# Moving the two split-weight buffers of a hybrid decoder layer by 80 bytes in SBUF

## The chip, the core and the metric

The kernel runs on one core of a Trainium2 chip. The metric is the device time of one launch in microseconds (us). Most runs of a kernel agree within 0.3%.

## What the reference computes

One inference step of a one-layer decoder, for 256 prompt tokens and 8 sample tokens (264 columns in all), in float32. The work is nearly all matrix products with weights that are read once:

```
x <- LN(a*x + 0.5*FFN1(x)); x <- LN(a*x + Mixer(x)); x <- LN(a*x + 0.5*FFN2(x))
swiglu(x) = (silu(x @ w_gate) * (x @ w_up)) @ w_down      # 2048 -> 5632 -> 2048
z = x @ w_in                                              # 2048 -> 10240: q,k,v | conv B,C,h | two gates
merged = sigmoid(g_attn) * (o @ w_attn_out) + sigmoid(g_conv) * (c_b*conv @ w_conv_out)
Mixer = merged @ w_o
```

Attention with two softmax maps per head, over the prompt and over a paged cache of 1024 positions for the 8 samples, lies between.

## The kernel before, in words

**Layout.** Features lie on the 128 partitions and the 264 tokens along each partition. An activation is a stack of tiles of 128 x 264 float32, 1056 bytes a partition each. Tile number kt is the kt-th block of 128 features.

**Split products.** Every float32 value is split into a high part of type float32r and a low remainder, and a product is made of three matmuls (`products`, lines 650 to 652): high weights by high activations (L650), high weights by low activations (L651), low weights by high activations (L652). The weight block, 128 x 128, is the stationary operand: its load is a record of its own (PEld), and the load for the next matmul runs beside the current matmul. The activation tile, 128 x 264, is the moving operand. So while one matmul streams its 264 columns out of one SBUF address, the load of the next reads 128 columns out of another.

**Weight pipeline.** Weights come in chunks of 256 rows x 512 columns (`KC` = 2 row blocks, `MC` = 4 column blocks), 512 KB each, by DMA from SyncE into the ring `w_raw` of 4 slots. ScalarE rounds a chunk into `w_hi` (L1004), VectorE subtracts and writes `w_lo` (L1382), TensorE runs 24 matmuls on it and then frees the slot (`w_used`). There are 752 chunks. A panel is a run of chunks that fills four PSUM banks: 8 chunks for products with x or m, 22 for the down projections (tiles `h_hi`, `h_lo`), 4 with `yc` or `o`. Within a chunk the order is row block, column block, the three products; in the last chunk of a panel column block comes first. The slot of a chunk is its running number modulo 4.

**Stages in order.** FFN1 gate and up: first the two panels side by side, chunk by chunk in turn (`side_by_side`, 16 chunks), then 20 panels one after another; down (4 panels with h); the query columns of `w_in` in two panels on activations not yet normalized (`first_panels`, tile `raw`, L764 to L766, 266 columns, 1064 bytes a tile); the rest of `w_in` with attention between; `w_conv_out` (tiles `yc`); `w_attn_out` (tiles `o`); `w_o` (tiles `m`); FFN2, which starts with two `raw` panels and then has 20 panels with x; down (4 panels with h). The two LayerNorm sums use small matmuls with the tile `ones`.

**Addresses.** A helper `at` places tensors one behind another at multiples of 32 bytes. The base that the allocator gives is byte 16,481 of the partition, so `x_hi` is at 16,512, `x_lo` at 33,408, `w_raw` at 50,304, `lam_in` at 66,688. Then `w_hi` is at 66,720 and `w_lo` at 83,360. A row of the split rings (one slot, one row block) is 512 columns and a gap of `W_GAP` = 8 columns that nobody uses, 2080 bytes. Later come small constants and LayerNorm tiles, and from `area`, rounded up to a multiple of `LINE` = 128 bytes, the large reused region: `h_hi` at 110,720, `h_lo` at 157,312, `m_hi` at 115,328, `o_hi` at 160,640, `raw` at 195,264, `yc_hi` at 202,752, `yc_lo` at 219,648. The matmuls read a weight block at

```
wh, wl = w_hi[:, s, k, m * P:(m + 1) * P], w_lo[:, s, k, m * P:(m + 1) * P]
```

that is at the ring's start + 2080 x (2s + k) + 512 m for slot s, row block k, column block m.

Of the kernel before, what the change touches and what calls it, by code (L numbers as in the profile page):

```python
# [20 lines left out]
F32R = mybir.dt.float32r  # L21
# [3 lines left out]
P = 128  # L25
# [5 lines left out]
HEADS, HD, VD = 8, 64, 128  # L31
# [3 lines left out]
KC, MC = 2, 4  # L35
RING = 4
LEAD = 3
WARM = 10
WC = MC * P
# [19 lines left out]
HEAD_STATS = 22  # L59
LATE = DT - MC  # L60
RAW = N + 2
LINE, W_GAP = 128, 8

class Count:
# [48 lines left out]
def program(nc, a, out):  # L114
    with ExitStack() as ctx:
# [4 lines left out]
        top = nc.sbuf_base  # L120
        end = nc.sbuf_usable_end

        def at(name, shape, dt=F32, offset=None):

            nonlocal top
            size = int(np.prod(shape[1:])) * 4
            if offset is None:
                top = -(-top // 32) * 32
                offset, top = top, top + size
            assert offset + size <= end, (name, offset, size, end)  # L130
            return nc.alloc_sbuf_tensor_at(name, shape, dt, offset=offset)
# [6 lines left out]
        y_norm = at("y_norm", [P, DT, N], F32, x_at + DT * TILE)  # L138
        w_raw = at("w_raw", [P, RING, KC, WC])
        lam_in = at("lam_in", [HD, 4])  # L140
        SPLIT_RING = RING * KC * (WC + W_GAP)
        w_at = -(-(top - 32) // LINE) * LINE + 32

        def spaced(flat):

            return flat[:].rearrange("p (s k n) -> p s k n", s=RING, k=KC)[:, :, :, 0:WC]

        w_hi = spaced(at("w_hi", [P, SPLIT_RING], F32R, w_at))
        w_lo = spaced(at("w_lo", [P, SPLIT_RING], F32R, w_at + SPLIT_RING * 4))
        top = w_at + (2 * SPLIT_RING - W_GAP) * 4  # L150
        lam_prod = at("lam_prod", [HD, 2])
        lam = at("lam", [P, 4])
        ident = at("ident", [P, P])
        ones = at("ones", [P, P])
        mask = at("mask", [P, 3, P])
# [53 lines left out]
        top = area  # L209
# [24 lines left out]
        top = max(top, zv_at + 6144 + (2 * PAD + SPLIT_COLS) * 4)  # L234
# [1820 lines left out]
```

## Time and profile before

| | |
|---|---|
| time, median of 3 runs | 2261.94 us (2261.67 to 2263.02) |
| the profiled execution: its own time | 2261.67 us |
| its span, first to last instruction | 2259.8 us |
| TensorE (PE) busy | 2243.9 us, 99% of the span |
| VectorE (DVE) / ScalarE (ACT) / GpSimd (POOL) busy | 1365.9 / 996.5 / 29.7 us |
| granted TensorE clock, mean | 0.998 of full |
| HBM read | 468 MB, 209 GB/s over the span |

Matmuls are pipelined: a matmul's record lasts some 280 ns, while the next one starts some 120 ns after it. What a matmul costs is the distance from start to start, which has to be read from start times; busy time does not show it.

### The profile page before, as it was taken

How to read it: one execution, taken by the hardware profiler on the slowest of the kernel's cores; microseconds unless marked ns; L12 is line 12 of the kernel's file. 1: busy time of each engine (PE TensorE's matmuls, PEld its weight loads, DVE VectorE, ACT ScalarE, POOL GpSimd, SP SyncE). 2: the span in 40 equal slices, each digit the busy share in tenths (PEclk: the TensorE clock that was granted, in tenths of full speed). 3: DMA queues.
4: the chain of work that ended last, by engine and by line, in shares of the span. 5: the costliest groups of instructions: out<-in, count | busy, mean ns of one | idle time of the engine just before them, and what ended most of it. 6: DMA issues, size and time to landing. Idle time of an engine off the chain costs nothing.

```text
span 2259.8 us, 45670 instructions
## 1 busy us (share of the span) xinstructions
PE 2243.9 (99%) x18574; PEld 2212.8 (98%) x18574; DVE 1365.9 (60%) x1523; ACT 996.5 (44%) x1236; POOL 29.7 (1%) x59
## 2 busy tenths in 40 slices
PE   9999999999999999999999999999999999999997
PEld 9999999999999999999998899999999999999997
DVE  5545454444655689999975447896444544445554
ACT  5444444433444454454543454554444434433333
POOL 1000000000000001000000000000000000000001
PEclk9999999999999999999999999999999999999999
DMA  7656666565555688989988855556656565655553
GB/s 246 195 177 186 179 183 183 176 188 181 182 180 182 189 283 291 318 290 323 331 310 312 296 182 189 185 175 189 181 176 189 174 191 176 186 185 180 179 185 114
DMA packets 233439, 475.47 MB, mean 210 GB/s; under 512 B 18448, under 2 KB 21888, under 8 KB 233312
## 3 DMA queue, kind: packets, MB, share of 16 engines
q1 hardware_dynamic: 225920, 465.22, 63.7%
q0 software_dynamic: 2320, 5.68, 0.8%
q10 hardware_dynamic: 5072, 2.78, 0.4%
q8 instruction: 93, 1.52, 0.3%
q14 instruction: 34, 0.28, 0.0%
HBM read 468.13 MB, written 4.43 MB: 209 GB/s over the span
## 4 chain that ended last, share of the span: by engine, by line
PE 95%; DVE 4%; DMA 0%; issue 0%; POOL 0%; ACT 0%; SPq 0%; DVEq 0%; ACTq 0%
PE ps L650 30%; PE ps L651 29%; PE ps L652 29%; PE ps L766 1%; PE ps L765 1%; PE ps L764 1%; DVE w_lo L1382 1%; PE ps L907 1%; DVE kv_ring L1714 1%; DVE scores L1720 1%; DMA kv_ring<-in_cache_v 0%; POOL y L633 0%; PE ps L795 0%; DMA w_raw<-in_ffn_w_gate 0%; PE ps L871 0%
## 5 line engine op out<-in xcount | busy, mean ns | idle before, releaser
L1382 DVE TENSOR_TENSOR w_lo<-w_raw,w_hi 128x1024 fp32r<-128x1024 f32 x750 | 912.4, 1223 | 790.5 <-ACT w_hi L1004 787.5
L1004 ACT ACTIVATE w_hi<-w_raw 128x1024 fp32r<-128x1024 f32 x750 | 789.3, 1058 | 1015.4 <-PE ps L652 972.6
L650 PE MATMUL ps<-x_hi,w_hi 128*128 128x264 f32 x3840 | 1089.6, 284 | 0.8 <-DVE w_lo L1442 0.8
L651 PE MATMUL ps<-x_lo,w_hi 128*128 128x264 f32 x3840 | 1084.7, 282 | 0.0
L652 PE MATMUL ps<-x_hi,w_lo 128*128 128x264 f32 x3840 | 1080.9, 281 | 0.0
L650 PEld LDWEIGHTS ps<-x_hi,w_hi 128*128 128x128 f32 x3840 | 719.9, 187 | 13.0 <-issue 7.7
L652 PEld LDWEIGHTS ps<-x_hi,w_lo 128*128 128x128 f32 x3840 | 721.4, 188 | 0.0
L651 PEld LDWEIGHTS ps<-x_lo,w_hi 128*128 128x128 f32 x3840 | 720.6, 188 | 0.0
L650 PE MATMUL ps<-h_hi,w_hi 128*128 128x264 f32 x1408 | 399.7, 284 | 0.0
L651 PE MATMUL ps<-h_lo,w_hi 128*128 128x264 f32 x1408 | 399.1, 283 | 0.0
L652 PE MATMUL ps<-h_hi,w_lo 128*128 128x264 f32 x1408 | 398.2, 283 | 0.0
L652 PEld LDWEIGHTS ps<-h_hi,w_lo 128*128 128x128 f32 x1408 | 264.6, 188 | 0.0
L651 PEld LDWEIGHTS ps<-h_lo,w_hi 128*128 128x128 f32 x1408 | 264.2, 188 | 0.1
L650 PEld LDWEIGHTS ps<-h_hi,w_hi 128*128 128x128 f32 x1408 | 264.1, 188 | 0.1
L1714 DVE TENSOR_TENSOR kv_ring<-kv_ring,q_bcast 128x1024 f32<-128x1024 f32 x64 | 77.8, 1216 | 1.2 <-DMA q_bcast<-q_scratch 1.2
L1720 DVE TENSOR_REDUCE scores<-kv_ring 128x16 f32<-128x1024 f32 x64 | 77.5, 1211 | 0.1
L764 PE MATMUL ps<-raw,w_hi 128*128 128x266 f32 x256 | 73.8, 288 | 0.0
L766 PE MATMUL ps<-raw,w_lo 128*128 128x266 f32 x256 | 73.3, 286 | 0.0
L765 PE MATMUL ps<-raw,w_hi 128*128 128x266 f32 x256 | 73.3, 286 | 0.0
L650 PE MATMUL ps<-m_hi,w_hi 128*128 128x264 f32 x256 | 72.6, 284 | 0.0
L651 PE MATMUL ps<-m_lo,w_hi 128*128 128x264 f32 x256 | 72.3, 282 | 0.0
L652 PE MATMUL ps<-m_hi,w_lo 128*128 128x264 f32 x256 | 72.0, 281 | 0.0
(268 smaller groups left out, 1367.9 us busy)
## 6 DMA issues: line engine op xcount, KB each, us to landing
w_raw<-in_ffn_w_down SPq DMA_DIRECT2D x176, 512.0 KB, 3.7
w_raw<-in_ffn_w_gate SPq DMA_DIRECT2D x175, 512.0 KB, 3.7
w_raw<-in_ffn_w_up SPq DMA_DIRECT2D x175, 512.0 KB, 3.8
w_raw<-in_w_in SPq DMA_DIRECT2D x160, 512.0 KB, 5.2
kv_ring<-in_cache_k SPq DMA_DIRECT2D x64, 512.0 KB, 6.1
kv_ring<-in_cache_v SPq DMA_DIRECT2D x64, 512.0 KB, 6.2
w_raw<-in_w_o SPq DMA_DIRECT2D x32, 512.0 KB, 4.2
w_raw<-in_w_conv_out SPq DMA_DIRECT2D x16, 512.0 KB, 5.5
```

Source lines behind the costliest of these rows:

```text
L650: nc.tensor.matmul(acc, wh, hi[:, kt], start=(kt == 0), stop=False)
L651: nc.tensor.matmul(acc, wh, lo[:, kt], start=False, stop=False)
L652: return nc.tensor.matmul(acc, wl, hi[:, kt], start=False, stop=last)
L764: nc.tensor.matmul(acc, wh, hi, start=(kt == 0), stop=False)
L765: nc.tensor.matmul(acc, wh, lo, start=False, stop=False)
L766: mm = nc.tensor.matmul(acc, wl, hi, start=False, stop=(kt == DT - 1))
L907: mm = nc.tensor.matmul(ps[rows, 6 + half], s_flat[:, at_page:at_page + P // SEQS].bitcast(F32), kv_ring[:, slots[k], half * WC:(half + 1) ...
L1004: nc.scalar.activation(w_hi[:, s], w_raw[:, s], ACT.Copy).then_inc(w_hi_ready, 1)
L1382: V.tensor_tensor(w_lo[:, s], w_raw[:, s], w_hi[:, s].bitcast(F32), ALU.subtract).then_inc(w_lo_ready, 1)
L1714: V.tensor_tensor(keys, keys, q_bcast[:, b % SEQS], ALU.mult).then_inc(k_mult, 1)
L1720: V.tensor_reduce(scores[:, j // PAGES, j % PAGES], keys.rearrange("p (g d) -> p g d", d=HD), AX, ALU.add).then_inc(k_free, 1)
```

## The change

Three edits, all to where tensors lie. The two small tensors `lam_prod` and `lam` move from behind the split rings to before them. The rings' allocation then begins at 66,784 (96 bytes past a multiple of 128), and four float32 columns, `W_FIRST`, are left free at the start of each, so that the first weight of `w_hi` is at 66,800 and that of `w_lo` at 83,440: both 80 bytes later than before. Tensors between the rings and `area` come to lie 32 bytes later. `area` and all behind it stay, and so do `x_hi`, `x_lo` and `w_raw`. No instruction is added, removed or reordered.

```diff
-LINE, W_GAP = 128, 8
+LINE, W_GAP, W_FIRST = 128, 8, 4
...
         lam_in = at("lam_in", [HD, 4])
-        SPLIT_RING = RING * KC * (WC + W_GAP)
-        w_at = -(-(top - 32) // LINE) * LINE + 32
-
-        def spaced(flat):
-
-            return flat[:].rearrange("p (s k n) -> p s k n", s=RING, k=KC)[:, :, :, 0:WC]
-
-        w_hi = spaced(at("w_hi", [P, SPLIT_RING], F32R, w_at))
-        w_lo = spaced(at("w_lo", [P, SPLIT_RING], F32R, w_at + SPLIT_RING * 4))
-        top = w_at + (2 * SPLIT_RING - W_GAP) * 4
         lam_prod = at("lam_prod", [HD, 2])
         lam = at("lam", [P, 4])
+        SPLIT_RING = RING * KC * (WC + W_GAP)
+        w_at = -(-(top + 32) // LINE) * LINE - 32
+
+        def spaced(flat):
+
+            return flat[:, W_FIRST:W_FIRST + SPLIT_RING].rearrange("p (s k n) -> p s k n", s=RING, k=KC)[:, :, :, 0:WC]
+
+        w_hi = spaced(at("w_hi", [P, W_FIRST + SPLIT_RING], F32R, w_at))
+        w_lo = spaced(at("w_lo", [P, W_FIRST + SPLIT_RING], F32R, w_at + SPLIT_RING * 4))
+        top = w_at + (W_FIRST + 2 * SPLIT_RING - W_GAP) * 4
         ident = at("ident", [P, P])
```

## Rows read from the trace of the kernel before

**Rows 1.** The page: its head, TensorE's busy time, the chain that ended last

```profile
span 2259.8 us, 45670 instructions
...
PE 2243.9 (99%) x18574; PEld 2212.8 (98%) x18574; DVE 1365.9 (60%) x1523; ACT 996.5 (44%) x1236; POOL 29.7 (1%) x59
...
PE 95%; DVE 4%; DMA 0%; issue 0%; POOL 0%; ACT 0%; SPq 0%; DVEq 0%; ACTq 0%
```

**Rows 2.** Tile w_lo's matmuls: count, duration ns min/median/max, first and last start, form

```profile
L652 PE MATMUL ps<-x_hi,w_lo x3840: 278/281/291, 6.3 to 1988.1; 128*128 128x264 f32 x192
...
L652 PE MATMUL ps<-h_hi,w_lo x1408: 278/282/288, 514.4 to 2244.3; 128*128 128x264 f32 x176
...
L766 PE MATMUL ps<-raw,w_lo x256: 279/286/293, 770.7 to 1526.7; 128*128 128x266 f32 x128
...
L652 PE MATMUL ps<-m_hi,w_lo x256: 280/281/283, 1385.8 to 1478.2; 128*128 128x264 f32 x128
...
L652 PE MATMUL ps<-yc_hi,w_lo x128: 278/285/290, 1171.3 to 1225.9; 128*128 128x264 f32 x128
...
L652 PE MATMUL ps<-o_hi,w_lo x128: 280/281/287, 1339.7 to 1385.5; 128*128 128x264 f32 x128
```

**Rows 3.** Timeline, TensorE: starts (first column, us) at panel ends, FFN1

```profile
52.80 0.29 PE L650 MATMUL ps<-x_hi,w_hi 128*128 128x264 f32 x1
...
514.14 0.29 PE L650 MATMUL ps<-h_hi,w_hi 128*128 128x264 f32 x1
...
642.54 0.28 PE L650 MATMUL ps<-h_hi,w_hi 128*128 128x264 f32 x1
...
705.95 0.28 PE L650 MATMUL ps<-h_hi,w_hi 128*128 128x264 f32 x1
...
770.34 0.28 PE L652 MATMUL ps<-h_hi,w_lo 128*128 128x264 f32 x1
```

**Rows 4.** Timeline, TensorE: every second chunk's first matmul, side-by-side panels

```profile
26.56 0.28 PE L650 MATMUL ps<-x_hi,w_hi 128*128 128x264 f32 x1
...
32.33 0.28 PE L650 MATMUL ps<-x_hi,w_hi 128*128 128x264 f32 x1
...
38.18 0.28 PE L650 MATMUL ps<-x_hi,w_hi 128*128 128x264 f32 x1
...
44.09 0.28 PE L650 MATMUL ps<-x_hi,w_hi 128*128 128x264 f32 x1
...
49.91 0.28 PE L650 MATMUL ps<-x_hi,w_hi 128*128 128x264 f32 x1
```

**Rows 5.** Timeline, TensorE: each chunk's first matmul, second raw panel, query projection

```profile
795.18 0.29 PE L764 MATMUL ps<-raw,w_hi 128*128 128x266 f32 x1
...
798.16 0.29 PE L764 MATMUL ps<-raw,w_hi 128*128 128x266 f32 x1
...
801.12 0.29 PE L764 MATMUL ps<-raw,w_hi 128*128 128x266 f32 x1
...
804.13 0.29 PE L764 MATMUL ps<-raw,w_hi 128*128 128x266 f32 x1
...
807.11 0.29 PE L764 MATMUL ps<-raw,w_hi 128*128 128x266 f32 x1
...
810.12 0.28 PE L764 MATMUL ps<-raw,w_hi 128*128 128x266 f32 x1
...
813.09 0.28 PE L764 MATMUL ps<-raw,w_hi 128*128 128x266 f32 x1
```

**Rows 6.** Timeline, ScalarE and VectorE in FFN1; idle time before it in brackets

```profile
200.05 1.06 ACT L1004 ACTIVATE w_hi<-w_raw 128x1024 fp32r<-128x1024 f32 x1 [1.82 <-PE ps L652]
...
201.14 1.23 DVE L1382 TENSOR_TENSOR w_lo<-w_raw,w_hi 128x1024 fp32r<-128x1024 f32 x1 [1.66 <-ACT w_hi L1004]
```

**Rows 7.** Groups by line: the two weight-split groups, count, busy us, mean ns, idle

```profile
L1382 DVE TENSOR_TENSOR w_lo<-w_raw,w_hi 128x1024 fp32r<-128x1024 f32 x750 | 912.4, 1223 | 790.5 <-ACT w_hi L1004 787.5 <-DVE y L1406 0.8 <-DVE z_c L1864 0.2
L1004 ACT ACTIVATE w_hi<-w_raw 128x1024 fp32r<-128x1024 f32 x750 | 789.3, 1058 | 1015.4 <-PE ps L652 972.6 <-DMA w_raw<-in_w_in 24.0 <-PE ps L766 8.6
```

## The prediction, on record before the result was seen

> **What bounds the kernel now.** I read the page first. TensorE is busy for 2243.9 of 2259.8 us and has 95% of the chain that ended last [rows 1]: nothing but the pace of its matmuls can move this kernel by much. Then the ScalarE and VectorE timelines, to see whether the weight split is near that pace: in a chunk of 24 matmuls ScalarE works 1.06 us and had stood idle 1.82 us before it, VectorE works 1.23 us after 1.66 us idle [rows 6]. So the pace is TensorE's own. Then I read start times, because durations hide the pace. From 52.80 to 514.14 us lie 3840 starts (20 panels of 192): 461.34/3840 = 120.1 ns a matmul [rows 3]. At the granted clock of 0.998 of the full 2.4 GHz, 264 columns stream in 110 ns, if one column goes per cycle (an estimate from the columns and the clock), so 10 ns of each matmul are something else.
>
> **What differs between stages.** The only thing that the change touches in TensorE's work is the address from which weight blocks are loaded, so the question is whether the trace shows that addresses matter. I call *distance* the address of a matmul's weight block minus that of its activation tile, modulo 256 bytes. In the x panels it is constant. Tile kt lies at 16,512 + 1056 kt, that is 128 + 32 kt modulo 256; the weight row 2s + k lies at 66,720 + 2080 (2s + k), that is 160 + 32 (2s + k); as a panel has 8 chunks, 2s + k and kt agree modulo 8, and the distance is 160 - 128 = 32, for the low tiles and low weights too (`x_lo` and `w_lo` lie whole multiples of 256 behind `x_hi` and `w_hi`). Column blocks are 512 bytes apart and drop out. `o` and `m` start at 128 modulo 256 as well: 32 again. In the down projections a panel has 22 chunks, so every second panel starts two slots (4 rows, 128 bytes) further on: distance 32, then 160, then 32, then 160. `yc` starts at 0 modulo 256: 160.
>
> The trace separates these. The third down panel, distance 32: (705.95 - 642.54)/528 = 120.1 ns. The fourth, distance 160, same code, same tiles: (770.34 - 705.95)/527 = 122.2 ns [rows 3]. Modulo 128 the two would be the same place, which is why I take 256. The matmuls on `yc` (160) last 285 ns in the median where those on x, `o` and `m` (32) last 281 [rows 2]. The side-by-side panels at the start visit four distances with identical work, 48 matmuls each: 32 takes (32.33 - 26.56)/48 = 120.2 ns, 96 takes 121.9, 160 takes 123.1, 224 takes 121.2 [rows 4]. So 32 is the best of the four, and the curve between them looks smooth with its top near 160.
>
> All those distances are multiples of 32. The new one is not: 66,800 is 240 modulo 256, so distance 32 becomes 112 and 160 becomes 240. Both are odd multiples of 16. Only the `raw` panels show such distances. A raw tile is 1064 bytes, so the distance falls by 16 from chunk to chunk for the even tiles (160, 144, 128, 112, 96, 80 in the first six chunks, high tiles), while the odd tiles start on no multiple of 16 at all. A chunk takes 2.98, 2.96, 3.01, 2.98, 3.01 and 2.97 us in this order [rows 5], over 24 that is 124.2, 123.3, 125.4, 124.2, 125.4 and 123.8 ns. It zigzags: 144, 112 and 80 are each shorter than their neighbours, by 1.5 (144), 1.2 (112) and 1.6 ns (80 against 96 alone), 1.4 in the mean. Only half of a raw chunk's matmuls have an even tile, so the matmuls at an odd multiple of 16 themselves would gain up to 2 x 1.4 = 2.8 ns.
>
> **The sum.** Matmuls by stage, three times the counts of [rows 2]: 3 x 3840 with x, of which 96 each at 96, 160 and 224 in the side-by-side panels, 3 x 1408 with h, half of them at 160, 768 with `m`, 384 each with `o` and `yc`. At distance 32: 11,232 + 2112 + 768 + 384 = 14,496. At 160: 2112 + 384 + 96 = 2592.
> - At 112, by the smooth curve, a quarter of the way from 121.9 to 122.2 (the long panel's value for 160): 122.0 ns. Less 2.8 for the odd multiple: 119.2. Against 120.1 that is -0.9 ns x 14,496 = -13 us.
> - At 240, a quarter of the way from 224 (121.2) to 32 (120.1): 120.9. Less 2.8: 118.1. Against 122.2 that is -4.1 ns x 2592 = -11 us.
> - The 768 raw matmuls: the chunks that lay at odd multiples of 16 go to even ones and the reverse; I take 0, with 1.4 ns x 768 = 1 us either way as the bound.
> - The remaining 192 side-by-side matmuls: under 1 us whatever happens, as 4 ns x 192 = 0.8.
>
> Sum -24 us on the profiled execution's 2261.7 us, which is 0.3 us from the median shown: 2238 us.
>
> **What I cost at nothing, and its cover.** ScalarE writes `w_hi` and VectorE reads and writes both rings at new offsets. 750 instructions of 1058 and 1223 ns [rows 7] have 1.7 to 1.8 us of idle time in front of each [rows 6], so each would have to more than double before TensorE waits. If it did, each further 0.1 us would cost 750 x 0.1 = 75 us. Nothing in the trace speaks for that: rows of the ring now begin at 32, 64, 96 and 0 modulo 128 in turn, and all take the same. The constants and LayerNorm tiles that move by 32 bytes serve a few dozen of 18,574 matmuls. The stall removed, if it is one, lies inside a matmul, so nothing becomes late next: DMA brings 512 KB a chunk in 2.88 us with a ring of four, and a chunk 0.02 us shorter asks for 1% more.
>
> One rule of the Trainium skill would give another sum. "SBUF — State Buffer", section "Who interferes with whom", gives TensorE two independent read ports, one for the moving operand and one for the weight load, and says that TensorE never waits on anyone. By it distance would not matter, and the sum would be 0. The trace disagrees: panels that differ in nothing but distance take 120.1 and 122.2 ns [rows 3].
>
> **Rivals.**
> - *Slower: the neighbours decide.* The zigzag in the raw panels comes from the odd tiles or the longer rows, not from the odd multiple of 16. Then 112 simply lies between 96 and 160, the worst part of the curve, at 122.0 ns: +1.9 x 14,496 = +28 us, while 240 at 120.9 gives -1.3 x 2592 = -3 us. 2262 + 25 = 2287 us. For it: 32 is the best distance that the trace has, and it is given up for the bulk. Against it: the zigzag holds five times in a row. It tips where the gain of the odd multiple falls under the (28 - 3)/17,088 = 1.5 ns that both shifts lose together; my 2.8 is a doubling of 1.4, and undoubled I would be within 2 us of no change, which is why this rival is strong.
> - *No change.* Either the half gain: 122.0 - 1.4 = 120.6 at 112, +7 us, and 120.9 - 1.4 = 119.5 at 240, -7 us; or distance is not what parts the panels at all, as the rule above has it. 2262 us. Against the second: three stages of different code agree on distance.
> - *Much faster.* The odd multiple takes 2.8 ns off each distance's own present level: -2.8 x 14,496 = -41 us, and with -11 us for the others 2210 us. This needs the good value of 32 to hold at 112 too, which nothing shows, but the floor of 110 ns leaves room.
>
> **Numbers.** A measurement of this kernel can tell about 0.2%, 4.5 us, from no change. Forecast (some 10 to 35 us faster) 0.37, much faster 0.13, no change 0.14, slower 0.36. The forecast gives 2238 us. The range takes in the slower rival at 2287 with a little for a top above 122.2 (160 took 123.1 side by side), and stops a little under the much faster case: 2208 to 2292. The forecast's own range is 2225 to 2253. Faster 0.50, same 0.14, slower 0.36.
>
> **What the profile after would show.** Start to start in FFN1's long stretch: 119.2 ns if I am right, 122.0 if the neighbours decide, 120.1 if distance does nothing; the stretch of 3840 starts would last 457.7, 468.5 or 461.3 us. The down panels would alternate between 119.2 and 118.1 ns. The raw zigzag would be turned over. ScalarE's and VectorE's durations should stay at 1058 and 1223 ns. I am wrong if the pace at 112 is set by something that distances in steps of 32, or tiles of another length, don't show: the value at 112 is inferred from chunks in which half the matmuls were something else, and that is the weakest step.

## The result and the profile after

The changed kernel takes 2274.76 us in the median of 6 runs (2274.2 to 2275.91), the kernel before 2262.32 us beside it. The ratio is 1.0055, 95% interval 1.0042 to 1.0068: 12.4 us slower. The time lies inside the range of the prediction (2208 to 2292), but on the other side of no change from its forecast of 2238 us.

The page of the changed kernel, its head, TensorE's busy time and the chain, answering to [rows 1]:

```profile
span 2272.6 us, 45670 instructions
...
PE 2258.4 (99%) x18574; PEld 2227.3 (98%) x18574; DVE 1366.7 (60%) x1523; ACT 998.0 (44%) x1236; POOL 29.8 (1%) x59
...
PE 99%; POOL 0%; DVE 0%; issue 0%; ACT 0%; DVEq 0%; POOLq 0%
```

The span grew by 12.8 us and TensorE is still the bound. Its share of the chain went from 95% to 99%. The two weight-split groups, by line, answering to [rows 7]:

```profile
L1382 DVE TENSOR_TENSOR w_lo<-w_raw,w_hi 128x1024 fp32r<-128x1024 f32 x750 | 912.9, 1223 | 799.0 <-ACT w_hi L1004 796.3 <-DVE y L1406 0.8 <-DVE z_c L1864 0.2
L1004 ACT ACTIVATE w_hi<-w_raw 128x1024 fp32r<-128x1024 f32 x750 | 790.4, 1060 | 1022.6 <-PE ps L652 987.6 <-DMA w_raw<-in_w_in 17.3 <-PE ps L766 7.3
```

Neither instruction got slower: 1223 and 1060 ns, against 1223 and 1058. Only their idle time grew: most of ScalarE's is a wait for TensorE's products (L652), 987.6 us against 972.6. The loss is in the pace of the matmuls. TensorE's timeline of the changed kernel, starts at the same panel ends as in [rows 3]:

```profile
52.60 0.28 PE L650 MATMUL ps<-x_hi,w_hi 128*128 128x264 f32 x1
...
518.43 0.28 PE L650 MATMUL ps<-h_hi,w_hi 128*128 128x264 f32 x1
...
646.87 0.29 PE L650 MATMUL ps<-h_hi,w_hi 128*128 128x264 f32 x1
...
710.89 0.28 PE L650 MATMUL ps<-h_hi,w_hi 128*128 128x264 f32 x1
...
774.77 0.28 PE L652 MATMUL ps<-h_hi,w_lo 128*128 128x264 f32 x1
```

The 3840 matmuls with x, now at distance 112, take (518.43 - 52.60)/3840 = 121.3 ns each, 1.2 more than before. The third down panel, also at 112, takes (710.89 - 646.87)/528 = 121.2 ns (before 120.1). The fourth, at 240, takes (774.77 - 710.89)/527 = 121.2 (before 122.2, at 160). So +1.2 x 14,496 - 1.0 x 2592 = +14.8 us, and the raw panels give back about half a microsecond. The span grew by 1.5 us less than that. Most of the difference is in the middle of the kernel, where the faster matmuls had to wait. TensorE in the stretch from 819 to 1339 us of the kernel before (first fence) and in the same stretch of the changed one (second fence), the windows view with busy us and count:

```profile
819.00:1339.00 520.00, 518.89 (x4293) 1.00 0.87 298
```

```profile
819.00:1339.00 520.00, 520.00 (x4271) 1.00 0.86 297
```

The kernel before idles 1.1 us there, its attention products waiting 0.7 us on VectorE and 0.4 on a page of the cache; the changed one does not wait. It also lacks a wait of 0.8 us for `w_lo` in the first 20 us, which the kernel before has. With the waits gone, VectorE's 4% left the chain.

### The profile page after: what moved, and what is told of

Its sections match the earlier page's. It is cut to its first block, busy times and chain, and to the rows that moved or that the text cites. A ratio compares the mean times of both kernels' runs of the same rounds, so it can differ in the third digit from the quotient of the medians.

```text
span 2272.6 us, 45670 instructions
## 1 busy us (share of the span) xinstructions
PE 2258.4 (99%) x18574; PEld 2227.3 (98%) x18574; DVE 1366.7 (60%) x1523; ACT 998.0 (44%) x1236; POOL 29.8 (1%) x59
## 4 chain that ended last, share of the span: by engine, by line
PE 99%; POOL 0%; DVE 0%; issue 0%; ACT 0%; DVEq 0%; POOLq 0%
PE ps L651 31%; PE ps L650 31%; PE ps L652 31%; PE ps L764 1%; PE ps L765 1%; PE ps L766 1%; PE ps L907 1%; POOL y L633 0%; PE ps L853 0%; PE ps L795 0%; PE ps L871 0%; PE ps L870 0%; PE ps L877 0%; PE ps L886 0%; PE ps L885 0%; PE ps L884 0%
## 5 line engine op out<-in xcount | busy, mean ns | idle before, releaser
L1382 DVE TENSOR_TENSOR w_lo<-w_raw,w_hi 128x1024 fp32r<-128x1024 f32 x750 | 912.9, 1223 | 799.0 <-ACT w_hi L1004 796.3
L1004 ACT ACTIVATE w_hi<-w_raw 128x1024 fp32r<-128x1024 f32 x750 | 790.4, 1060 | 1022.6 <-PE ps L652 987.6
L652 PE MATMUL ps<-x_hi,w_lo 128*128 128x264 f32 x3840 | 1094.1, 285 | 0.0
L650 PEld LDWEIGHTS ps<-x_hi,w_hi 128*128 128x128 f32 x3840 | 726.5, 189 | 12.4 <-issue 8.2
L652 PEld LDWEIGHTS ps<-x_hi,w_lo 128*128 128x128 f32 x3840 | 726.1, 189 | 0.0
L652 PE MATMUL ps<-h_hi,w_lo 128*128 128x264 f32 x1408 | 400.4, 284 | 0.0
L652 PEld LDWEIGHTS ps<-h_hi,w_lo 128*128 128x128 f32 x1408 | 265.7, 189 | 0.0
L652 PE MATMUL ps<-m_hi,w_lo 128*128 128x264 f32 x256 | 72.9, 285 | 0.0
```

Source lines behind the costliest of these rows:

```text
L650: nc.tensor.matmul(acc, wh, hi[:, kt], start=(kt == 0), stop=False)
L652: return nc.tensor.matmul(acc, wl, hi[:, kt], start=False, stop=last)
L1004: nc.scalar.activation(w_hi[:, s], w_raw[:, s], ACT.Copy).then_inc(w_hi_ready, 1)
L1382: V.tensor_tensor(w_lo[:, s], w_raw[:, s], w_hi[:, s].bitcast(F32), ALU.subtract).then_inc(w_lo_ready, 1)
```

## The experiments

For each kernel I give its time beside runs of the kernel before on the same chip (2262.2 to 2262.6 us), and the two paces read from its own timeline: start to start over the 3840 matmuls with x in FFN1 (*bulk*, the distance of 14,496 matmuls) and over the fourth down panel (*other*, the distance of 2592, always 128 more). The time of a kernel comes from several runs, its paces from the one profiled execution.

The rows of the rings start at all eight multiples of 32 modulo 256, and so do the tiles of x and h. So a move of the rings by a multiple of 32 changes only which row meets which tile; a move by an odd multiple of 16 also puts the weight blocks on new places.

### Does the distance set the pace, and with what period?

The first three move the rings by placing small constants before them. `area` and the activation tiles stay. For e1 (two constants in front, and four free columns) the core of the edit is

```diff
+        lam_prod = at("lam_prod", [HD, 2])
+        conv_w = at("conv_w", [P, 3, AT])
...
-        w_at = -(-(top - 32) // LINE) * LINE + 32
+        w_at = -(-top // 32) * 32
...
-            return flat[:].rearrange("p (s k n) -> p s k n", s=RING, k=KC)[:, :, :, 0:WC]
+            return flat[:, 4:4 + SPLIT_RING].rearrange("p (s k n) -> p s k n", s=RING, k=KC)[:, :, :, 0:WC]
```

The other two have no leading columns; e4 has the same two constants there, e2 five small tensors.

> Rings moved by 144 bytes instead of 80: distance 176 for x, o, m and half of h; 48 for yc and the other half. Weight blocks still start at odd multiples of 16. Theory A (the distance modulo 256 between weight block and activation tile sets the pace): the side-by-side panels of the changed kernel took 120.3 ns at 176 and 121.5 at 48, so 14,496 matmuls lose 0.2 ns and 2592 gain 0.7 against before: 2262 + 3 - 2 = 2263 us. Theory B (it is the weight block's own start at an odd multiple of 16 that costs): as the changed kernel, 2275 us. Theory C (tensors that were moved beside the rings, or ScalarE and VectorE writing them at an odd multiple of 16): 2275 us too.

Measured: 2258.03 us, ratio 0.998 (0.997 to 0.9989), a little faster than both kernels and 5 us below the sum. Its timeline:

```profile
52.64 0.28 PE L651 MATMUL ps<-x_hi,w_hi 128*128 128x264 f32 x1
...
514.25 0.28 PE L651 MATMUL ps<-h_hi,w_hi 128*128 128x264 f32 x1
...
705.08 0.29 PE L651 MATMUL ps<-h_hi,w_hi 128*128 128x264 f32 x1
...
768.48 0.29 PE L653 MATMUL ps<-h_hi,w_lo 128*128 128x264 f32 x1
```

Bulk (distance 176) 461.61/3840 = 120.2 ns, other (48) 63.40/527 = 120.3 ns. Weight blocks that start at an odd multiple of 16 cost nothing by themselves: theory B falls. The sum undersold it, since 48 in a long panel takes 120.3 and not the 121.5 of the side-by-side chunks; that is 3 of the 5 us.

> Rings moved by 256 bytes, small tensors placed before them: every distance modulo 256 is that of before (32 and 160), all constants and LayerNorm tiles are moved. Theory A: start to start 120.1 ns in the x panels as before, 2262 us within 2. If the period is 512 or longer: anything else. Theory C (the moved small tensors cost): 2275 us.

Measured: 2262.33 us, ratio 1.0 (0.9991 to 1.001); bulk 120.1, other 122.2 ns. All of the moved tensors together cost nothing (theory C in its first form falls; in its second form, the writes of ScalarE and VectorE, it fell with e1), and a whole 256 bytes changes nothing.

> Rings moved by 128 bytes: the two distances of before change places, 160 for x, o, m and half of h, 32 for yc and the other half. All starts at multiples of 32. Theory A: 14,496 matmuls go from 120.1 to 122.2 ns (+30 us), 2592 from 122.2 to 120.1 (-5 us): 2287 us. Theory B: no odd multiple of 16, so 2262 us.

Measured: 2284.37 us, ratio 1.0096 (1.008 to 1.0113). The two paces change places:

```profile
52.48 0.28 PE L651 MATMUL ps<-x_hi,w_hi 128*128 128x264 f32 x1
...
521.44 0.29 PE L651 MATMUL ps<-h_hi,w_hi 128*128 128x264 f32 x1
...
714.38 0.28 PE L651 MATMUL ps<-h_hi,w_hi 128*128 128x264 f32 x1
...
777.67 0.28 PE L653 MATMUL ps<-h_hi,w_lo 128*128 128x264 f32 x1
```

Bulk (160) 468.96/3840 = 122.1 ns, other (32) 63.29/527 = 120.1 ns. With the kernel before this is the clearest evidence for the distance: the same two values on exchanged stages, from weight rows that start at the same places modulo 256. The two panels read the same rings while the same engines write into them, so no moved tensor and no writing engine explains the difference; and since it changes sides, neither does the panels' place or their PSUM banks. The sum of 2287 us was 3 us too high.

The fourth moves everything, so that no distance changes:

```diff
-            return nc.alloc_sbuf_tensor_at(name, shape, dt, offset=offset)
+            whole = nc.alloc_sbuf_tensor_at(name, [shape[0], MOVE + size // 4], dt, offset=offset)[:, MOVE:]
...
+            if len(shape) > 2:
+                whole = whole.rearrange(f"p ({axes}) -> p {axes}", **sizes)
+            return whole
```

with `MOVE` = 4 columns.

> Every tensor of the kernel before is moved by 16 bytes, so that all distances stay as before but all weight blocks and all activation tiles start at odd multiples of 16. Theory A: 2262 us within 2, 120.1 ns in the x panels. Theory B: 2275 us or more, 121.3 ns or more. Theory C in its second form (ScalarE and VectorE writing at odd multiples of 16): longer than 1058 and 1223 ns, and 2275 us.

Measured: 2259.81 us, ratio 0.9988 (0.9979 to 0.9998).

```profile
52.38 0.28 PE L655 MATMUL ps<-x_hi,w_hi 128*128 128x264 f32 x1
...
514.21 0.28 PE L655 MATMUL ps<-h_hi,w_hi 128*128 128x264 f32 x1
...
705.21 0.28 PE L655 MATMUL ps<-h_hi,w_hi 128*128 128x264 f32 x1
...
768.50 0.28 PE L657 MATMUL ps<-h_hi,w_lo 128*128 128x264 f32 x1
```

Bulk (32) 461.83/3840 = 120.3 ns, but other (160) 63.29/527 = 120.1 ns, not 122.2. The third down panel, again at 32, takes 120.7 ns, although the first takes 120.1. So distance is not the whole story: with both operands at odd multiples of 16 the bad distance 160 is as good as the best, and theory A's 120.1 ns at 32 no longer holds in every panel. ScalarE and VectorE, which here write at odd multiples of 16 too, take no longer (1059 and 1222 ns in the mean, 1058 and 1223 before). Theory A is shown only for tiles that start where those of the kernel before do.

### The map

Four more kernels, made in the same way, fill in the distances at steps of 16.

> Rings moved by 48 bytes: distance 80 for 14,496 matmuls, 208 for 2592, weight blocks at odd multiples of 16. Smooth curve through the odd multiples measured so far (48: 120.3, 112: 121.2, 176: 120.1, 240: 121.2 ns): 120.8 at 80, 120.7 at 208, so 2262 + 0.7 x 14,496 - 1.5 x 2592 = 2268 us. Rival (each step of 32 has its own value, with no curve between them): anything from 120.0 to 122.5 ns, that is 2255 to 2297 us.

> Rings moved by 112 bytes: distance 144 for the bulk, 16 for the others, odd multiples of 16. Smooth curve: 120.7 at 144 and at 16, so 2262 + 0.6 x 14,496 - 1.5 x 2592 = 2267 us. Rival (no curve): 2255 to 2297 us.

> Rings moved by 32 bytes: distance 64 for the bulk, 192 for the others, multiples of 32. Smooth curve through 32 (120.1), 96 (121.9), 160 (122.2), 224 (121.4): 121.0 at 64 and 121.8 at 192, so 2262 + 0.9 x 14,496 - 0.4 x 2592 = 2274 us. Rival (no curve): 2255 to 2297 us.

> Rings moved by 224 bytes: distance 0 for the bulk, 128 for the others, multiples of 32. Smooth curve: 120.7 at 0 and 122.1 at 128, so 2262 + 0.6 x 14,496 = 2271 us. A rival in which weight load and activation stream disturb each other most when they start at the same place: more than the 122.2 ns of distance 160, so over 2287 us.

And the change taken apart: p1 is its 16 bytes alone, p2 its 64 bytes alone.

> One part of the change alone: the 16 bytes in front of the rings (W_FIRST), without the 64 bytes. Distance 48 for the bulk, 176 for the others. From the panels that had these distances in e1 (120.3 at 48, 120.1 at 176): 2262 + 0.2 x 14,496 - 2.0 x 2592 = 2260 us, so no loss at all. Rival (odd multiples of 16 cost by themselves): 2270 us or more.

> The other part alone: rings 64 bytes later, W_FIRST = 0. Distance 96 for the bulk, 224 for the others. From the side-by-side chunks of before (121.9 and 121.3 ns): 2262 + 1.8 x 14,496 - 0.9 x 2592 = 2286 us, so a bigger loss than the whole change, of which the 16 bytes take some back. Rival (the 64 bytes do nothing since they are whole lines of 32): 2262 us.

| kernel | rings moved by | time, us | ratio (95%) | bulk: distance, ns | other: distance, ns |
|---|---|---|---|---|---|
| before | 0 | 2262.3 | | 32, 120.1 | 160, 122.2 |
| p1 | 16 | 2261.1 | 0.9995 (0.9986 to 1.0004) | 48, 120.4 | 176, 120.1 |
| s3 | 32 | 2282.0 | 1.0087 (1.007 to 1.0104) | 64, 121.8 | 192, 121.1 |
| s1 | 48 | 2287.8 | 1.0111 (1.0094 to 1.0128) | 80, 122.3 | 208, 121.6 |
| p2 | 64 | 2284.6 | 1.0097 (1.0081 to 1.0112) | 96, 121.9 | 224, 121.7 |
| the change | 80 | 2274.8 | 1.0055 (1.0042 to 1.0068) | 112, 121.3 | 240, 121.2 |
| s2 | 112 | 2284.7 | 1.0098 (1.0081 to 1.0115) | 144, 122.0 | 16, 121.3 |
| e4 | 128 | 2284.4 | 1.0096 (1.008 to 1.0113) | 160, 122.1 | 32, 120.1 |
| e1 | 144 | 2258.0 | 0.998 (0.997 to 0.9989) | 176, 120.2 | 48, 120.3 |
| s4 | 224 | 2279.9 | 1.0077 (1.006 to 1.0094) | 0, 121.8 | 128, 120.2 |

There is no curve. The pace lies between 120.1 and 122.3 ns; it is low at 32 and 48, at 128 and at 176, and it goes from 120.2 to 122.0 and back to 120.2 within 48 bytes (128, 144, 176, with 160 at 122.1 between). The mean of the eight odd multiples of 16 is 121.3 ns, that of the eight even ones 121.3 too. The expectation of a smooth curve missed all four of the s kernels; the rival, each step has its own value, was not contradicted, but its range of 2255 to 2297 us left it little to be wrong about. What did forecast well were paces taken over from panels at the same distance: 2260 us for p1 (measured 2261.1) and 2286 us for p2 (2284.6). The parts of the change do not add up: 16 bytes cost nothing, 64 cost 22 us, both together 12.

### Is the loss paid when the row changes?

Cut into runs of 12 matmuls on one weight row, the changed kernel seemed to lose its time around a change of row: in all chunks but the last of the same 20 panels, the second to fourth steps of a run take 123.7, 124.7 and 121.5 ns and the last 123.2, the others 119.9 to 120.5. The changed kernel with the two loops exchanged:

```diff
-                    for k, m in itertools.product(range(KC), range(MC)):
+                    for m, k in itertools.product(range(MC), range(KC)):
```

> The changed kernel with column block outside and row block inside in every chunk, as its last chunks have it already: the row (and with it activation tile and weight row) then changes after 3 matmuls instead of 12. Theory D (at distance 112 the pace is 120.0 ns inside a row, and what is lost is lost after each change of row, some 16 cycles of 1.2 GHz per change in the changed kernel's profile): as in its last chunks, 122.2 ns everywhere, +1.0 x 12,700 at 112 and +0.8 x 2500 at 240: 2275 + 15 = 2290 us. If the loss is spread evenly over all matmuls: 2275 us. If each change of row costs its 16 cycles again: 16/3 = 5 cycles or 4.4 ns a matmul more than 120.0, so 124.4 ns and 2320 us.

Measured: 2276.3 us, 1.5 us from the changed kernel.

```profile
52.54 0.28 PE L650 MATMUL ps<-x_hi,w_hi 128*128 128x264 f32 x1
...
517.87 0.28 PE L650 MATMUL ps<-h_hi,w_hi 128*128 128x264 f32 x1
```

465.33/3840 = 121.2 ns: four times as many changes of row, and no more loss in the bulk. There theory D, which wanted 122.2 ns, fell. In the down panels at the same distance it did not: the third goes from 121.2 to (711.57 - 647.00)/528 = 122.3 ns.

```profile
647.00 0.29 PE L650 MATMUL ps<-h_hi,w_hi 128*128 128x264 f32 x1
...
711.57 0.28 PE L650 MATMUL ps<-h_hi,w_hi 128*128 128x264 f32 x1
```

So the order can matter, and why it does in one stage and not in the other is open. A pace that each change of row sets alone is ruled out by the bulk. The same idea in the raw panels, on the kernel of e1 (row block outside, column block inside in `first_panels`):

> The fastest kernel so far (distance 176, e1), with row block outside and column block inside in the raw panels, so that a row serves 12 matmuls there instead of 3. Theory D, weakened: raw panels fall from 123.4 ns towards the 120.9 that 266 columns at the pace of 264 would give: up to -2.5 x 770 = -2 us, 2256 us. If changes of row cost nothing, as r1 says of distance 112: 2258 us.

Measured: 2258.52 us, ratio 0.9981 (0.9972 to 0.999), e1's time. The bulk stays at 120.2 ns, the second raw panel at e1's 123.4 ns a matmul, and nothing is gained. In the bulk and in the raw panels, changes of row are not where the time is.

### What are the 120 ns?

The kernel before with fewer columns in the products. For r3 (the two corrections on 256 columns):

```diff
-                nc.tensor.matmul(acc, wh, lo[:, kt], start=False, stop=False)
-                return nc.tensor.matmul(acc, wl, hi[:, kt], start=False, stop=last)
+                nc.tensor.matmul(acc[:, 0:T], wh, lo[:, kt, 0:T], start=False, stop=False)
+                return nc.tensor.matmul(acc[:, 0:T], wl, hi[:, kt, 0:T], start=False, stop=last)
```

r5 and r4 have 256 and 128 columns in all three products, except the first of each bank. The products for the other tokens are left out there, so their results are wrong; everything behind still runs, on incomplete sums. Loads, weights and order are unchanged.

> The kernel before, with the two correction products (low activations by high weights, high activations by low weights) on the 256 prompt columns only: the 8 sample tokens go without these corrections. The weight loads are unchanged, two of three matmuls stream 8 columns fewer. If the moving stream sets the 120.0 ns: 8/2.4 = 3.3 ns less on two of three, mean 117.8 ns in the x panels, 2262 - 2.2 x 17,280 = 2224 us. If the weight load sets it: 120.0 ns, 2262 us or a few us beside it as the pattern of disturbances changes.

> As the first of these, with 256 columns instead of 128. If load and stream share a resource by bytes (264 + 128 columns take 144 cycles of 1.2 GHz, as 392 x 0.367): 384 columns take 141 cycles, 117.6 ns. If the load sets the pace: 120.0 ns. If the stream sets it: 116.7 ns.

> The kernel before, with all matmuls of the 264-column form (but the first product of a bank, which writes all columns) on 128 columns only: most of the computation for the other tokens is left out. Weight loads unchanged. If the load of 128 x 128 weights sets the pace: 120.0 ns stays, 2262 us. If stream and load share something, so that only their sum counts: the pace falls well under 120, to some 107 to 112 ns (128 columns at 1.2 per ns), 2050 to 2130 us. If the stream alone set it: 60 ns, and another engine would bound.

> The same edit on the changed kernel (distances 112 and 240). If the loss at distance 112 comes from the stream and the load reading at the same time: with a stream half as long there is less to collide, and the pace is that of the kernel above within 0.3 ns. If it comes from the weight load alone (its start at an odd multiple of 16): the 1.2 ns stay between the two kernels, 15 us or more.

Measured: r3 2246.31 us (0.9929, 0.9913 to 0.9944), bulk 119.4 ns; r5 2228.5 us (0.9851, 0.9836 to 0.9867), bulk (504.26 - 51.47)/3840 = 117.9 ns. Neither forecast for r3 (2224 or 2262 us) and none for r5 (117.6, 120.0 or 116.7 ns) was hit; for r5 117.6 came nearest. The first r4 kernel ran twice, in 2200.8 and 2844.5 us, the second in 2203.0 and 2204.8 us. I take no verdict from these times and read only the profiled executions, of 2199.0 and 2201.2 us span. The forecast of 2050 to 2130 us from their pace was missed: between 800 and 1200 us their granted clock is 0.78, and 0.958 over the span. In the stretch that I read it is 1.00. TensorE between 100 and 400 us, of r4 on the kernel before and of r4 on the changed kernel, and for comparison of the changed kernel itself:

```profile
100.00:400.00 300.00, 300.00 (x2685) 1.00 0.64 195
```

```profile
100.00:400.00 300.00, 300.00 (x2684) 1.00 0.64 195
```

```profile
100.00:400.00 300.00, 300.00 (x2475) 1.00 0.57 180
```

2685 and 2684 matmuls in 300 us: 111.7 ns a matmul, those of the first products with 264 columns among them, and one matmul in 2685 apart between distance 32 and 112, as was expected if a short stream has less to collide with. In the unchanged kernels 24 matmuls part them (2499 before, 2475 after). A neighbourhood of matmuls that all have 128 columns, in r4 on the kernel before:

```profile
200.98 0.28 PE L652 MATMUL ps<-x_lo,w_hi 128*128 128x128 f32 x1
...
202.43 0.27 PE L653 MATMUL ps<-x_hi,w_lo 128*128 128x128 f32 x1
```

13 steps in 1.45 us: 111.5 ns, although 128 columns would stream in 53 (128 / 2.4, the estimate of the prediction). Nearly the same, then, as the 110 ns that 264 columns would need for the stream alone. What is left to explain 111.5 ns is the weight load, which is unchanged, or a fixed cost of every matmul; no run has a load without a stream or the reverse, so that it is the load is argued, not shown.

Distance 32 against 160 can be read inside these kernels too, from the third and the fourth down panel. First r4 on the kernel before, then r5:

```profile
597.10 0.33 PE L651 MATMUL ps<-h_hi,w_hi 128*128 128x264 f32 x1
...
656.09 0.34 PE L651 MATMUL ps<-h_hi,w_hi 128*128 128x264 f32 x1
...
714.98 0.28 PE L653 MATMUL ps<-h_hi,w_lo 128*128 128x128 f32 x1
```

```profile
630.52 0.28 PE L651 MATMUL ps<-h_hi,w_hi 128*128 128x264 f32 x1
...
692.77 0.28 PE L651 MATMUL ps<-h_hi,w_hi 128*128 128x264 f32 x1
...
756.24 0.28 PE L653 MATMUL ps<-h_hi,w_lo 128*128 128x256 f32 x1
```

## Why the prediction was wrong

- *TensorE's pace is all that can move the kernel*: right. ScalarE and VectorE kept 1060 and 1223 ns, and the moved constants cost nothing (e2).
- *The distance between weight block and tile, modulo 256, sets the pace*: right where it was used, by e2 and e4, and the numbers for 32 and 160 held to 0.1 ns. It is not complete: at distance 160 a move of everything by 16 bytes gives 120.1 for 122.2 ns (e3).
- *"Less 2.8 for the odd multiple"*: this step failed. In the panels that the sum is about there is no such gain: the mean of odd and even multiples is the same in the map, 121.3 ns, and beside the curve's 122.0 and 120.9 the change measured 0.7 ns less and 0.3 ns more, where the sum had 2.8 less both times. The zigzag of [rows 5] was taken from raw tiles, and it does not carry over. In the raw panels themselves something of it is real: over the first six chunks of the second and fourth raw panel, in the kernel before, the changed one and the nine others that move the rings and no more, chunks with even tiles at an odd multiple take 123.2 ns a matmul and the others 124.2. But that is 0.9 ns and not 1.4, and it does not alternate in every kernel. The changed kernel's second raw panel, every chunk's first matmul, even tiles now at 240, 224, 208, 192, 176 and 160:

```profile
799.52 0.28 PE L764 MATMUL ps<-raw,w_hi 128*128 128x266 f32 x1
...
802.46 0.29 PE L764 MATMUL ps<-raw,w_hi 128*128 128x266 f32 x1
...
805.40 0.28 PE L764 MATMUL ps<-raw,w_hi 128*128 128x266 f32 x1
...
808.31 0.29 PE L764 MATMUL ps<-raw,w_hi 128*128 128x266 f32 x1
...
811.27 0.28 PE L764 MATMUL ps<-raw,w_hi 128*128 128x266 f32 x1
...
814.23 0.29 PE L764 MATMUL ps<-raw,w_hi 128*128 128x266 f32 x1
...
817.21 0.28 PE L764 MATMUL ps<-raw,w_hi 128*128 128x266 f32 x1
```

  2.94, 2.94, 2.91, 2.96, 2.96, 2.98 us: the zigzag that was forecast turned over is gone, though the odd multiples (240, 208, 176) are still 0.02 us shorter in the mean. I had read a rule for all tiles out of five differences in one mixed stage, and doubled it because only half of the matmuls were of the kind; the doubling alone turned "no change" into -24 us. Why raw tiles, of which every second starts on no multiple of 16, show it and the others don't is open.
- *"By the smooth curve"*: wrong as well, though it cost less; at 112 it was too high by 0.7 ns, which took back a quarter of the error of the 2.8. It gave 122.0 at 112 (measured 121.3) and 120.9 at 240 (measured 121.2). Four points at steps of 64 bytes can't show a thing that changes at steps of 16.
- *The sum*: -0.9 and -4.1 ns were forecast, +1.2 and -1.0 measured; -13 and -11 us became +17 and -3. That the measured time lies inside the range is owed to the slower rival, which the range had to take in, and not to the sum.
- *The slower rival* (neighbours decide, +25 us) had the right sign and twice the size. Its mechanism, a smooth curve without a gain, is not what the map shows. Its distance 96, in p2, does lose 22 us.
- *No change because the ports are independent*: ruled out. The Trainium skill, "SBUF — State Buffer", says in "Who interferes with whom" that TensorE never waits on anyone. The runs disagree: addresses alone make 30 us between e1 and s1.
- The Trainium skill, "TensorE: Matmul & The Clock Gate", says in "Back-to-back issue gap" that in a stream of weight loads and matmuls both set the spacing. The runs with fewer columns agree as far as they go: 111.7 ns where the stream alone would need some 53, and 120 where it would need some 110 (estimates from the columns and the clock).

What stays open: why one distance gives 120.1 and its neighbour 122. That it is stream and load reading at the same time which disturb each other is argued, not shown. It fits that the distance counts at 256 and 264 columns and not at 128, but at 128 some other limit of 111.7 ns may simply hide such a loss. e3 says that a full account needs the start of both operands, not only their difference, and r1 that it needs the order.

## What to carry to other kernels

When TensorE is the bound and weights are reloaded for each matmul, try where in SBUF the stationary operand lies relative to the moving one. Here it was worth up to 1.3% (2258 to 2288 us), although only 0.2% against this kernel's own start. Equal row pitches modulo 256 (1056 and 2080 bytes here) keep the relation the same for every tile of a panel. Then measure all sixteen steps of 16 bytes: no value tells its neighbour's, but a value read from a panel at one distance forecast other kernels at that distance well (p1 from e1's panels, p2 from the side-by-side chunks). Read the pace from start times over thousands of matmuls: durations and busy time barely show it. Don't turn a pattern seen in one mixed stage into a term of a sum without a second stage that shows it clean.

## What the runs showed of the hardware

- A 264-column float32r matmul with its weight load takes 120.1 ns in the long panels at the best distances (before, e4) and 122.3 at the worst (s1). With 256 columns it takes 117.9 or 120.4 ns, at distance 32 or 160 (r5), with 128 columns 111.7 at either (r4).
- Moving both operands by 16 bytes is not neutral: distance 160 went from 122.2 to 120.1 ns (e3).
- A shift of the weights by 256 bytes is neutral to 0.1 ns in both paces (e2).
